# A shift that follows as a bias: the first two projection blocks from rows without the additive part of the modulation

## The chip, the cores and the metric

The kernel runs on one core of one Trainium2 chip. The metric is the device time in microseconds of one execution; lower is better. A profile of one execution is read beside it.

## The reference

A transformer block with adaptive modulation is followed by two more blocks (a short convolution mixer and a dilated attention mixer, each with its feed-forward part), on 256 tokens of width 1024 in float32. Only the start matters here:

```
mod = silu(c) @ w_ada + b_ada          # c: 1 x 1024, w_ada: 1024 x 6144
shift1, scale1, gate1, shift2, scale2, gate2 = split(mod, 6)
h    = rms_norm(x, norm1_w) * (1 + scale1) + shift1
proj = h @ w_in                        # 1024 x 2832
gq, gk, gv, gz, ga, gb, sq, sk, sv = split(proj, ...)
qkv  = silu(causal_depthwise_conv(concat([gq, gk, gv]), conv_w))   # 4 taps
```

After it come a chunked gated delta rule on q, k and v, a sliding window attention, the output projection and the feed-forward part. Scale and shift are the same for all tokens, so h @ W is (x_normed * (1 + scale1)) @ W plus the column shift1 @ W.

## The kernel before

Features lie on the partitions, tokens in the free dimension. x is eight tiles of 128 features x 256 tokens. All weights come in blocks of 1024 rows x 256 columns (1 MB), one after the other through a ring of three buffers (`raw`). For float32 accuracy each block is split: ScalarE writes a rounded high part (`hi(w)`, L650), VectorE the rest (`lo(w)`, L1017), and TensorE multiplies high by high, high by low and low by high (`three`, L1615 is the line of every product). One block of a projection is 8 row tiles x 2 column halves x 3 = 48 products.

Each engine runs its own hand-written list of instructions; semaphores join them. Around the change the order is this.

SyncE issues the two halves of x, then four transfers of modulation weights (`load_ada(0, 0..3)`), weight blocks 0 and 1, four more modulation transfers as their buffers come free (`load_ada(1, 0..3)`), and after the third of these has landed the rest of the weight blocks. A modulation transfer has half of the 1024 input rows and 512 output columns; `half` 0 are the columns for features 0 to 511, `half` 1 those for 512 to 1023, of the scale (i = 0, 1) and of the shift (i = 2, 3).

TensorE multiplies each with silu(c) (`ada`), four rows of partial results at once. ScalarE copies them to SBUF (`mod_rows_copy`, L689), and TensorE turns and sums them with products of one column (`row_sums`). VectorE makes from them the factor a1 (`first_scales`) and the shift (`first_shifts`), then for each of four row tiles `first_scaled` (times a1 plus shift), ScalarE's high part (`h_high`, L676) and the low part (`first_low`, L1069). x was multiplied by the reciprocal root mean square first (L1125).

So TensorE's order is: `ada`, sums of squares, `ada`, the root's broadcast, `ada`, `row_sums`, `ada`, `row_sums`, with ten products on zeros between (`warm`); block 0, rows 0 to 3 (`column_half`); the four products of the second half; block 1, rows 0 to 3; block 0, rows 4 to 7; the gate product `gab` and a T5 product; block 1, rows 4 to 7; then blocks 2 to 10 one by one. The first six blocks go through a causal convolution: ScalarE copies the block to `pad` (L724), VectorE does four taps on each of two tiles (L1171 the first, L1178 the others), ScalarE applies SiLU (`feature`, L712) and, for queries and keys, squares the result (L715). The second part of the modulation (gate1 and others) is not made on TensorE: VectorE accumulates eight blocks with `accumulate` (L1032, L1034), whose place in the load order stands in `MOD_AT`.

Of the kernel before, what the change touches and what calls it, by code (L numbers as in the profile page):

```python
# [43 lines left out]
MOD_AT = ((0, 8), (9, 1), (10, 1), (W_OUT, 2 + EARLY_BLOCKS), (W_OUT + 2, 2), (LOOP_W, 6 - EARLY_BLOCKS)) + tuple((FFN_BASE[0] + 3 * j + 2, 1) for j in (2, 3, 4, 5))  # L44
# [10 lines left out]
STREAM_ORDER.sort()  # L55

# [111 lines left out]
class Semaphores:  # L168


    def __init__(self, new):
# [5 lines left out]
        self.x_scaled = new("x_scaled")  # L177
# [41 lines left out]
        self.t_ready = new("t_ready")  # L219
        self.h_hi_ready = new("h_hi_ready")  # L220
# [14 lines left out]
        self.pad_ready = new("pad_ready")  # L235
        self.conv_done = new("conv_done")
# [76 lines left out]
def build(nc, stream, x_in, consts_in, vectors_in, gab_in, t5_onehot, t5_log, rel_bias, out):  # L313
    t5_scratch = nc.dram_tensor("t5_scratch", (16, 384), F32, kind="Internal")
    with ExitStack() as ctx:
# [51 lines left out]
        with ExitStack() as one:  # L367
# [14 lines left out]
            second_ident = p1("second_ident", [P, HALF])  # L382
            gab_w = p1("gab_w", [P, KD * 16])
# [149 lines left out]
        def _(sp):  # L533
# [9 lines left out]
            def load_ada(half, i):  # L543
                if half:
                    sp.wait_ge(s.ada_used, i + 1)
                k, c = 4 * (i % 2), 512 * half + (D if i < 2 else 0)
                sp.dma_start(ada_raw[i].rearrange("p (k c) -> p k c", k=4),
                             stream[k:k + 4, :, c:c + 512].rearrange("k p c -> p k c")).then_inc(ada_landed[i], 16)
# [80 lines left out]
        def _(act):  # L629
# [40 lines left out]
            def h_high(n, ks=range(KD)):  # L670
                for k in ks:
                    act.wait_ge(s.t_ready, 8 * n + k + 1)
                    if n:
                        act.activation(normed(n)[0][:, k, :], nt[:, k, :], ACT.Identity, bias=shift2[:, k:k + 1]).then_inc(s.h_hi_ready, 1)
                    else:
                        act.activation(normed(n)[0][:, k, :], nt[:, k, :], ACT.Copy).then_inc(s.h_hi_ready, 1)  # L676
# [10 lines left out]
            def mod_rows_copy(half, u):  # L687
                act.wait_ge(s.ada_used, 4 * half + 2 * u + 2)
                act.activation(mod_rows[half][u], B[u][:, :], ACT.Copy).then_inc(s.rows_copied, 1)  # L689

            mod_rows_copy(0, 0)
            r = weight_load(0)
            act.wait_ge(raw_landed[r % RING], (r // RING + 1) * 16)
            for q in range(4):
                act.activation(high_of(0)[:, 2 * q:2 * q + 2, :], raw_of(r)[:, 2 * q:2 * q + 2, :], ACT.Copy).then_inc(s.first_hi, 1)
                if q == 1:
                    mod_rows_copy(0, 1)
            hi(1)
            h_high(0, range(4))
# [3 lines left out]
            mod_rows_copy(1, 0)  # L703
            mod_rows_copy(1, 1)
            h_high(0, range(4, KD))


            dest = [kT[:, 0:2, :], kT[:, 2:4, :], qT[:, 0:2, :], qT[:, 2:4, :], vT[:, 0:2, :], vT[:, 2:4, :]]

            def feature(w):  # L710
                act.wait_ge(s.conv_done, w + 1)
                act.activation(dest[w], cacc.rearrange("p (a b) -> p a b", a=2), ACT.Silu).then_inc(s.feature_ready, 1)  # L712
                if w < 4:
                    act.wait_ge(s.feature_ready, w + 1)
                    act.activation(head_sq[w].rearrange("p (a b) -> p a b", a=2), dest[w], ACT.Square).then_inc(s.head_squared, 1)  # L715

            for w in range(6):
                hi(w + 2)
# [5 lines left out]
                act.activation(pad[:, :, 3:259], A[w % 4].rearrange("p (a b) -> p a b", a=2), ACT.Copy).then_inc(s.pad_ready, 1)  # L724
                if w:
                    feature(w - 1)
                if w == 0:
                    act.wait_ge(s.gab_product, 1)
                    act.activation(gabT, B[0][0:16, 0:T], ACT.Copy).then_inc(s.gab_copied, 1)
                if w == 2:  # L730
# [275 lines left out]
        def _(dve):  # L1006
# [56 lines left out]
            def first_scaled(k):  # L1063
                dve.wait_ge(s.x_scaled, k + 1)
                dve.tensor_scalar(nt[:, k, :], nt[:, k, :], a1[:, k:k + 1], mods[:, k:k + 1], ALU.mult, ALU.add).then_inc(s.t_ready, 1)

            def first_low(k):
                dve.wait_ge(s.h_hi_ready, k + 1)
                dve.tensor_tensor(h_lo[:, k, :], nt[:, k, :], h_hi[:, k, :], ALU.subtract).then_inc(s.h_lo_ready, 1)  # L1069

            def first_scales(half):
                c, at = slice(4 * half, 4 * half + 4), 480 + 8 * half
                dve.wait_ge(s.rows_summed, 2 * half + 1)
# [3 lines left out]
            def first_shifts(half):  # L1077
                c, at = slice(4 * half, 4 * half + 4), 484 + 8 * half
                dve.wait_ge(s.rows_summed, 2 * half + 2)
                dve.tensor_tensor(mods[:, c], STAT[:, at:at + 4], vecs("b_ada")[:, c], ALU.add).then_inc(s.mod_ready, 1)  # L1080
                dve.wait_ge(s.mod_ready, 2 * half + 2)
# [41 lines left out]
            dve.wait_ge(s.rstd_ready, 1)  # L1123
            for k in range(KD):
                dve.tensor_tensor(nt[:, k, :], x[:, k, :], B[3][:, 256:512], ALU.mult).then_inc(s.x_scaled, 1)  # L1125
# [8 lines left out]

            first_scales(0)
            first_lows((0, 1))
            first_shifts(0)
            for k in range(4):
                first_scaled(k)
                if k:  # L1140
                    first_low(k - 1)
            first_low(3)
            first_lows((2, 3))
            lo(1)
            dve.wait_ge(s.gab_hi, 1)
            dve.tensor_tensor(gab_wl[:, :], gab_w[:, :], gab_wh[:, :], ALU.subtract).then_inc(s.gab_lo, 1)
            first_scales(1)
            first_shifts(1)
            for k in range(4, KD):
                first_scaled(k)  # L1150
                if k > 4:
                    first_low(k - 1)
            first_low(KD - 1)


            for w in range(6):
# [5 lines left out]
                lo(w + 2)  # L1162
                if w < 6:
                    dve.wait_ge(s.pad_ready, w + 1)
                    if w:
                        dve.wait_ge(s.feature_ready, w)
                    tile0 = (4, 6, 0, 2, 8, 10)[w]
                    for mt in range(2):
                        o = cacc[:, 256 * mt:256 * mt + 256]
                        cw = V_AT["conv_w"][0] + 4 * (tile0 + mt)  # L1170
                        dve.tensor_scalar(o, pad[:, mt, 0:256], vec[:, cw:cw + 1], None, ALU.mult).then_inc(s.dve_step, 1)  # L1171
                        steps[0] += 1
                    for tap in range(1, 4):
                        for mt in range(2):
                            o = cacc[:, 256 * mt:256 * mt + 256]
                            cw = V_AT["conv_w"][0] + 4 * (tile0 + mt) + tap
                            dve.wait_ge(s.dve_step, steps[0] - 1)
# [8 lines left out]
                if w == 1:  # L1186
# [9 lines left out]
                if w == 2:  # L1196
# [30 lines left out]
            accumulate(at)  # L1227
            at += 1
# [8 lines left out]
            dve.tensor_scalar(v8(coefq[:, :]), hsv[:, :, 8:16], HD ** -0.5, None, ALU.mult).then_inc(s.coef_ready, 1)  # L1237

# [374 lines left out]
        def _(pe):  # L1613
# [16 lines left out]
            def column_half(w, bank, ks, after_one=None):  # L1630

                if w or ks[0]:
                    pe.wait_ge(s.lo_ready, w + 1)
                wh = high_of(w)
                wl = low_of(w)
                for k in ks:
                    if k == 1 and after_one is not None:
                        after_one()
# [4 lines left out]
                    pe.wait_ge(s.h_lo_ready, k + 1)  # L1643
# [4 lines left out]
                if ks[-1] == KD - 1:  # L1648
                    ins.then_inc(s.block_used, 1)
# [90 lines left out]
            def ada(half, i):  # L1740

                pe.wait_ge(ada_landed[i], 16 * (half + 1))
                if half and i % 2 == 0:
                    pe.wait_ge(s.rows_copied, 1 + i // 2)
# [685 lines left out]
```

## Time and profile before

| | us |
|---|---|
| median of 3 runs | 1009.4 (1009.29 to 1013.27) |
| the profiled execution | 1015.11 |
| its span, first to last instruction | 1013.3 |
| TensorE busy (matmul) | 978.1 |
| VectorE busy | 611.0 |
| ScalarE busy | 476.1 |
| mean granted clock, share of full | 0.985 |

The profiled execution is longer than the median by 5.7 us; durations below come from it. A row of a timeline gives the start, the length from the first start to the last end of a merged group, the engine, the line, what is written from what, the count, and in brackets how long the engine had been idle and what ended that. Matmul ends are modelled, so the distance between starts says more than a duration. A float32 product counts as two instructions, a product of split parts as one.

### The profile page before, as it was taken

The page shows a single profiled execution, that of the slowest core. Times are in us where ns is not written, and L with a number is a line of the kernel's source. Part 1 is how long each engine was busy: PE and PEld are TensorE (multiplying, and loading weights), DVE is VectorE, ACT ScalarE, POOL GpSimd, SP SyncE. Part 2 cuts the span into 40 slices and gives each one's busy share as a digit, 9 for nine tenths or more (in the row PEclk, how much of TensorE's full clock was granted, in tenths as well). Part 3 has the DMA queues.
Part 4 walks back from the last instruction along what each step waited for, and adds up shares of the span by engine and source line. Part 5 has one row for each costly group of instructions (what it writes and reads, how often), then busy time and mean ns, then how long its engine had stood idle before and what let it go on. Part 6 is the DMA issues. An engine that isn't in the chain of part 4 may idle for free.

```text
span 1013.3 us, 15242 instructions
## 1 busy us (share of the span) xinstructions
PE 978.1 (97%) x6518; PEld 845.1 (83%) x6518; DVE 611.0 (60%) x749; ACT 476.1 (47%) x635; POOL 35.8 (4%) x36
## 2 busy tenths in 40 slices
PE   5799999999999999999999999999999999999997
PEld 3699988988878888899878888888999878888885
DVE  2488998865656454687664536364776564545453
ACT  3376358445334344534273434345645473535342
POOL 0000542000000000000000000000000000000000
PEclk9799999989999999999999999999999999999998
DMA  9746422756675546265544555554544255454521
GB/s 344 282 154 223 167 85 90 287 209 248 233 265 216 199 142 231 84 250 183 192 164 168 185 190 187 187 190 143 208 156 142 78 188 186 163 211 170 204 83 41
DMA packets 31554, 185.66 MB, mean 183 GB/s; under 512 B 3008, under 2 KB 5504, under 8 KB 10752
## 3 DMA queue, kind: packets, MB, share of 16 engines
q1 hardware_dynamic: 29952, 180.37, 49.4%
q0 software_dynamic: 832, 3.17, 1.0%
q10 hardware_dynamic: 704, 1.17, 0.3%
q8 instruction: 51, 0.84, 0.3%
q14 instruction: 15, 0.12, 0.0%
HBM read 183.62 MB, written 1.07 MB: 182 GB/s over the span
## 4 chain that ended last, share of the span: by engine, by line
PE 78%; DVE 11%; DMA 4%; ACT 4%; issue 2%; POOL 0%; SPq 0%; ACTq 0%; DVEq 0%
PE bank L1615 42%; PE acc L1615 33%; DVE w_lo L1017 3%; ACT w_hi L650 3%; DMA raw<-stream 2%; DMA keys_queries<-stream 2%; PE bank L2197 2%; DVE XT L1178 1%; DMA AT<-stream 1%; PE bank L1979 1%; DVE h_parts L1454 0%; DVE keys_queries L1034 0%; DVE XT L1309 0%; PE acc L1715 0%; PE bank L1715 0%
## 5 line engine op out<-in xcount | busy, mean ns | idle before, releaser
L1017 DVE TENSOR_TENSOR w_lo<-raw,w_hi 128x2048 fp32r<-128x2048 f32 x145 | 329.4, 2289 | 161.3 <-ACT w_hi L650 160.8
L1615 PE MATMUL bank<-w_hi,h_parts 128*128 128x512 f32 x1056 | 334.8, 392 | 3.2 <-DVE w_lo L1017 2.4
L650 ACT ACTIVATE w_hi<-raw 128x2048 fp32r<-128x2048 f32 x145 | 272.7, 1907 | 94.0 <-PE acc L1615 62.0
L1615 PEld LDWEIGHTS bank<-w_hi,h_parts 128*128 128x128 f32 x1056 | 199.2, 189 | 46.1 <-DVE w_lo L1017 3.2
L1615 PE MATMUL bank<-w_lo,h_parts 128*128 128x512 f32 x528 | 206.2, 391 | 0.0
L1615 PE MATMUL acc<-h_parts,w_hi 128*128 128x256 f32 x928 | 174.6, 290 | 3.1 <-DVE h_parts L1069 2.1
L1615 PEld LDWEIGHTS acc<-h_parts,w_hi 128*128 128x128 f32 x928 | 147.1, 195 | 7.7 <-issue 6.1
L1615 PE MATMUL acc<-h_parts,w_lo 128*128 128x256 f32 x464 | 133.2, 287 | 0.0
L1615 PE MATMUL acc<-w_hi,o_hi 128*128 128x512 f32 x296 | 118.9, 402 | 0.0
L1615 PEld LDWEIGHTS bank<-w_lo,h_parts 128*128 128x128 f32 x528 | 99.6, 189 | 20.2
L1615 PE MATMUL acc<-w_hi,o_lo 128*128 128x512 f32 x296 | 115.6, 391 | 0.0
L1615 PE MATMUL acc<-w_lo,o_hi 128*128 128x512 f32 x296 | 115.5, 390 | 0.0
L1615 PEld LDWEIGHTS acc<-h_parts,w_lo 128*128 128x128 f32 x464 | 90.3, 195 | 0.0
L1483 DVE TENSOR_TENSOR o_lo<-bank,o_hi 128x512 fp32r<-128x512 f32 x33 | 22.8, 691 | 79.3 <-ACT o_hi L892 79.1
L887 ACT ACTIVATE silu_and_hid<-bank,rms 128x256 f32<-128x256 f32 x44 | 20.9, 475 | 104.2 <-PE bank L1615 104.2
L1615 PEld LDWEIGHTS acc<-w_hi,o_lo 128*128 128x128 f32 x296 | 55.6, 188 | 12.3
L1615 PEld LDWEIGHTS acc<-w_hi,o_hi 128*128 128x128 f32 x296 | 55.6, 188 | 10.9 <-issue 0.2
L1615 PEld LDWEIGHTS acc<-w_lo,o_hi 128*128 128x128 f32 x296 | 55.7, 188 | 10.6
L892 ACT ACTIVATE o_hi<-bank 128x512 fp32r<-128x512 f32 x33 | 19.8, 599 | 77.3 <-PE bank L2197 77.3
L1475 DVE SCALAR_TENSOR_TENSOR silu_and_hid<-bank,rms,silu_and_hid 128x256 f32<-128x256 f32 x44 | 21.2, 481 | 33.0 <-ACT silu_and_hid L887 33.0
L1615 PE MATMUL bank<-h_parts,w_hi 128*128 128x256 f32 x192 | 34.9, 286 | 0.0
L1615 PEld LDWEIGHTS bank<-h_parts,w_hi 128*128 128x128 f32 x192 | 29.7, 190 | 0.2 <-issue 0.2
(365 smaller groups left out, 973.1 us busy)
## 6 DMA issues: line engine op xcount, KB each, us to landing
raw<-stream SPq DMA_DIRECT2D x162, 1024.0 KB, 5.0
AT<-stream SPq DMA_DIRECT2D x2, 1024.0 KB, 12.0
qkT<-stream SPq DMA_DIRECT2D x2, 1024.0 KB, 11.8
X_inv<-stream SPq DMA_DIRECT2D x2, 1024.0 KB, 13.0
keys_queries<-stream SPq DMA_DIRECT2D x2, 1024.0 KB, 15.1
t_tables<-t_scratch POOLq DMA_DIRECT2D x1, 2048.0 KB, 12.1
x_res<-x_in SPq DMA_DIRECT2D x2, 512.0 KB, 5.2
t_tables<-t_scratch POOLq DMA_DIRECT2D x1, 1024.0 KB, 14.5
```

The lines of the kernel that those rows point to most:

```text
L650: act.activation(high_of(w), raw_of(r), ACT.Copy).then_inc(s.hi_ready, 1)
L887: act.activation(sg[:, T * t:T * t + T], B[t][:, 0:256], ACT.Silu, scale=rms[:, t:t + 1] if f else 1.0).then_inc(s.silu_ready, 1)
L892: act.activation(hid_parts(j)[0].rearrange("p a b -> p (a b)"), B[2][:, :], ACT.Copy).then_inc(s.hid_hi_ready, 1)
L1017: dve.tensor_tensor(low_of(w), raw_of(weight_load(w)), high_of(w), ALU.subtract).then_inc(s.lo_ready, 1)
L1178: ins = dve.scalar_tensor_tensor(out=o, in0=pad[:, mt, tap:tap + 256], scalar=vec[:, cw:cw + 1], in1=o, op0=ALU.mult, op1=ALU.add)
L1475: dve.scalar_tensor_tensor(out=o, in0=up, scalar=rms[:, t:t + 1], in1=gate, op0=ALU.mult, op1=ALU.mult).then_inc(s.hid_ready, 1)
L1483: dve.tensor_tensor(low.rearrange("p a b -> p (a b)"), B[2][:, :], high.rearrange("p a b -> p (a b)"), ALU.subtract).then_inc(s.hid_lo_rea ...
L1615: return pe.matmul(o, l, r, start=start, stop=stop, skip_group_check=True)
L1979: ins = pe.transpose(bank[hh][:, P * i:P * i + P], sc[:, hh, P * i:P * i + P], perm)
L2197: ins = pe.transpose(B[2][:, T * i + P * t:T * i + P * t + P], hid[:, T * t + P * i:T * t + P * i + P], ident)
```

## The change

It has five parts.

- The first two blocks are multiplied with "plain" rows, x times root times a1, without the shift (`first_scaled` is now one operation from x; `plain_high`, `plain_low`). TensorE also multiplies their weights with the shift (`shift_products`: two columns, the shift's high and low part, each with the high and the low part of the weights, 32 products for each block). A reduction adds these up to `first_bias`, and ScalarE adds it when it copies the two blocks to `pad`. After the last plain product (`plain_used`) ScalarE and VectorE write the rows anew with the shift in them, for all later blocks.
- The transfers come as scale, scale (features 0 to 511), block 0, scale, scale (512 to 1023), block 1, shift, shift, block 2, shift, shift. TensorE's order follows; `row_sums` works by halves of 64 columns.
- Both parts of block 2 are made before the loop over the blocks, and the gate and T5 products come after block 2.
- The first convolution tap goes from VectorE to ScalarE (`first_tap`).
- The first two loads of the second part of the modulation both stand behind block 9, and the first `accumulate` stands behind the coefficients.

```diff
-MOD_AT = ((0, 8), (9, 1), (10, 1), (W_OUT, 2 + EARLY_BLOCKS), ...
+MOD_AT = ((0, 8), (10, 2), (W_OUT, 2 + EARLY_BLOCKS), ...
@@ SyncE
-            for i in range(4):
-                load_ada(0, i)
+            load_ada(0)
+            load_ada(1)
             load(0)
+            load_ada(2)
+            load_ada(3)
             load(1)
-            for i in range(4):
-                load_ada(1, i)
-            sp.wait_ge(ada_landed[2], 32)
-            for i in range(2, len(LOADS)):
+            load_ada(4)
+            load_ada(5)
+            load(2)
+            load_ada(6)
+            load_ada(7)
+            for i in range(3, len(LOADS)):
                 load(i)
@@ ScalarE
+            def plain_high(ks):
+                for k in ks:
+                    act.wait_ge(s.t_ready, k + 1)
+                    act.activation(h_hi[:, k, :], nt[:, k, :], ACT.Copy).then_inc(s.plain_hi, 1)
...
+            plain_high(range(4))
+            mod_rows_copy(1)
             hi(1)
-            h_high(0, range(4))
+            plain_high(range(4, KD))
...
-            mod_rows_copy(1, 0)
-            mod_rows_copy(1, 1)
-            h_high(0, range(4, KD))
+            mod_rows_copy(2)
+            act.wait_ge(s.mod_ready, 3)
+            act.activation(shift_parts[:, 0:4, 0], mods[:, 0:4], ACT.Copy).then_inc(s.shift_hi, 1)
+            hi(2)
+            mod_rows_copy(3)
+            act.wait_ge(s.mod_ready, 4)
+            act.activation(shift_parts[:, 4:8, 0], mods[:, 4:8], ACT.Copy).then_inc(s.shift_hi, 1)
+            act.wait_ge(s.plain_used, 1)
+            for k in range(KD):
+                act.activation(h_hi[:, k, :], nt[:, k, :], ACT.Identity, bias=mods[:, k:k + 1]).then_inc(s.h_hi_ready, 1)
...
+            def first_tap(w):
+                act.wait_ge(s.pad_ready, w + 1)
+                for mt in range(2):
+                    cw = V_AT["conv_w"][0] + 4 * (CONV_TILES[w] + mt)
+                    ins = act.activation(cacc[:, 256 * mt:256 * mt + 256], pad[:, mt, 0:256], ACT.Copy, scale=vec[:, cw:cw + 1])
+                ins.then_inc(s.tap_ready, 1)
...
+                if w < 2:
+                    act.wait_ge(s.bias_ready, 1)
+                    for mt in range(2):
+                        ins = act.activation(pad[:, mt, 3:259], A[w][:, 256 * mt:256 * mt + 256], ACT.Identity,
+                                             bias=first_bias[:, 2 * w + mt:2 * w + mt + 1])
+                    ins.then_inc(s.pad_ready, 1)
@@ VectorE
+            first_lows((0, 1))
             first_scales(0)
-            first_lows((0, 1))
-            first_shifts(0)
+            dve.wait_ge(s.rstd_ready, 1)
             for k in range(4):
                 first_scaled(k)
...
             first_lows((2, 3))
+            first_scales(1)
+            for k in range(4, KD):
+                first_scaled(k)
+                if k > 4:
+                    plain_low(k - 1)
+            plain_low(KD - 1)
             lo(1)
...
+            first_shifts(0)
+            lo(2)
             first_shifts(1)
+            dve.wait_ge(s.plain_used, 1)
+            for k in range(KD):
+                first_low(k)
+            dve.wait_ge(s.block_used, 2)
+            dve.tensor_reduce(first_bias[:, :], A[3][:, 0:8].rearrange("p (n two) -> p n two", two=2), AX.X, ALU.add).then_inc(s.bias_ready, 1)
@@ TensorE
+            def shift_products(w, ks):
+
+                wh, wl = high_of(w), low_of(w)
+                pe.wait_ge(s.shift_lo, ks[-1] // 4 + 1)
+                for k in ks:
+                    for mt in range(2):
+                        c, o = slice(P * mt, P * mt + P), A[3][:, 4 * w + 2 * mt:4 * w + 2 * mt + 2]
+                        mm(o, wh[:, k, c], shift_parts[:, k, :], w + k + mt == 0, False)
+                        ins = mm(o, wl[:, k, c], shift_parts[:, k, :], False, k == KD - 1)
+                return ins
...
+            ada(0)
             sums(0)
+            ada(1)
             rstd(0)
+            row_sums(0)
+            ada(2)
             warm(4)
+            column_half(0, A[0], range(4))
+            ada(3)
+            warm(2)
+            row_sums(1)
             warm(6)
+            column_half(0, A[0], range(4, KD))
+            ada(4)
+            ada(5)
+            column_half(1, A[1], range(4))
+            row_sums(2)
+            ada(6)
+            ada(7)
+            column_half(1, A[1], range(4, 6))
+            shift_products(0, range(4))
+            row_sums(3)
+            column_half(1, A[1], range(6, KD)).then_inc(s.plain_used, 1)
+            shift_products(1, range(4))
+            shift_products(0, range(4, KD)).then_inc(s.block_used, 1)
+            shift_products(1, range(4, KD)).then_inc(s.block_used, 1)
```

## Rows read from the trace of the kernel before

**Rows 1.** The page: TensorE's busy time, its clock by slices, the chain's shares.
```profile
PE 978.1 (97%) x6518; PEld 845.1 (83%) x6518; DVE 611.0 (60%) x749; ACT 476.1 (47%) x635; POOL 35.8 (4%) x36
...
PEclk9799999989999999999999999999999999999998
...
PE 78%; DVE 11%; DMA 4%; ACT 4%; issue 2%; POOL 0%; SPq 0%; ACTq 0%; DVEq 0%
```

**Rows 2.** TensorE's waits, 0 to 140 us: total us, times, longest.
```profile
PE bank L1615 <- DMA AT<-stream: 10.5, 1, 10.5
PE bank L1615 <- DMA keys_queries<-stream: 2.2, 1, 2.2
PE acc L1615 <- DVE h_parts L1069: 2.1, 1, 2.1
PE bank L1615 <- DMA X_inv<-stream: 0.9, 1, 0.9
PE bank L1615 <- DVE coefq L1237: 0.7, 1, 0.7
```

**Rows 3.** Timeline of TensorE, 20 to 57 us: start, length, group, idle before.
```profile
20.33 1.05 PE L1615 MATMUL bank<-consts,inv_b 128*128 128x1 f32 x8
...
28.31 0.40 PE L1615 MATMUL acc<-h_parts,w_hi 128*128 128x256 f32 x2
...
28.67 0.40 PE L1615 MATMUL acc<-h_parts,w_hi 128*128 128x256 f32 x2
...
31.77 1.04 PE L1615 MATMUL bank<-qkT,c_columns 128*32 128x512 f32 x8
...
34.70 1.05 PE L1615 MATMUL bank<-consts,inv_b 128*128 128x1 f32 x8
37.93 1.93 PE L1615 MATMUL bank<-keys_queries,c_columns 128*32 128x512 f32 x8 [2.18 <-DMA keys_queries<-stream]
...
41.24 1.70 PE L1615 MATMUL bank<-consts,inv_b 128*128 128x1 f32 x8
42.80 0.78 PE L1615 MATMUL acc<-h_parts,w_hi 128*128 128x256 f32 x2
...
49.80 0.40 PE L1615 MATMUL bank<-h_parts,gab_wh 128*16 128x256 f32 x2
...
53.45 0.51 PE L1615 MATMUL acc<-h_parts,w_hi 128*128 128x256 f32 x2
...
56.71 0.51 PE L1615 MATMUL acc<-h_parts,w_hi 128*128 128x256 f32 x2
```

**Rows 4.** Timeline of TensorE near 198 us: one-column products.
```profile
197.79 2.03 PE L1615 MATMUL bank<-consts,keys_queries 128*64 128x1 f32 x64
```

**Rows 5.** Busy time by stretches of 2 us; PEclk, DMA share and GB/s last.
```profile
36.00:38.00 2.00, 0.07 (x4) 0.07 (x8) 0.15 (x1) 0.00 (x0) 0.00 (x0) 0.72 1.01 422
...
46.00:48.00 2.00, 2.00 (x14) 2.00 (x14) 0.62 (x2) 1.74 (x1) 0.00 (x0) 0.72 0.00 0
...
198.00:200.00 2.00, 2.00 (x66) 1.99 (x63) 1.69 (x4) 1.70 (x2) 0.00 (x0) 1.00 0.01 4
200.00:202.00 2.00, 2.00 (x14) 2.00 (x14) 1.28 (x2) 2.00 (x2) 0.00 (x0) 0.68 0.03 8
...
204.00:206.00 2.00, 2.00 (x19) 2.00 (x18) 1.26 (x1) 0.00 (x0) 0.00 (x0) 0.96 0.97 287
```

**Rows 6.** Timeline of VectorE, 42 to 97 us.
```profile
42.98 0.16 DVE L1080 TENSOR_TENSOR mods<-bank,vec 128x4 f32<-128x4 f32 x1 [6.83 <-PE bank L1615]
...
55.09 2.29 DVE L1017 TENSOR_TENSOR w_lo<-raw,w_hi 128x2048 fp32r<-128x2048 f32 x1 [1.47 <-ACT w_hi L650]
59.25 0.62 DVE L1171 TENSOR_SCALAR XT<-inv_p,vec 128x256 f32<-128x256 f32 x2 [1.87 <-ACT keys_queries L712]
59.78 2.46 DVE L1178 SCALAR_TENSOR_TENSOR XT<-inv_p,vec,XT 128x256 f32<-128x256 f32 x6
...
96.10 0.69 DVE L1241 TENSOR_TENSOR keys_queries<-keys_queries,bank 128x512 f32<-128x512 f32 x1 [1.20 <-PE bank L1615]
```

More of the change, by code:

```diff
@@ L219, in __init__ @@
         self.t_ready = new("t_ready")
+        self.plain_hi = new("plain_hi")
+        self.plain_lo = new("plain_lo")
+        self.plain_used = new("plain_used")
+        self.shift_hi = new("shift_hi")
+        self.shift_lo = new("shift_lo")
+        self.bias_ready = new("bias_ready")
         self.h_hi_ready = new("h_hi_ready")
@@ L235, in __init__ @@
         self.pad_ready = new("pad_ready")
+        self.tap_ready = new("tap_ready")
         self.conv_done = new("conv_done")
@@ L672, in h_high @@
                     act.wait_ge(s.t_ready, 8 * n + k + 1)
[L673 to L676, printed above, removed]
+                    act.activation(normed(n)[0][:, k, :], nt[:, k, :], ACT.Identity, bias=shift2[:, k:k + 1]).then_inc(s.h_hi_ready, 1)
             act.wait_ge(s.vectors_loaded, 16)
@@ L1628, in three, with column_half @@
                 return mm(o, wl, xh, False, last)
-            def column_half(w, bank, ks, after_one=None):
-                if w or ks[0]:
-                    pe.wait_ge(s.lo_ready, w + 1)
+            def column_half(w, bank, ks):
                 wh = high_of(w)
                 wl = low_of(w)
+                if w:
+                    pe.wait_ge(s.lo_ready, w + 1)
                 for k in ks:
-                    if k == 1 and after_one is not None:
-                        after_one()
                     if w == 0 and k in (0, 2, 4):
@@ L1738, in _, with ada, row_sums @@
             two = lambda b: b[:, :].rearrange("p (a b) -> p a b", a=2)
[L1740 to L1744, printed above, removed]
+            def ada(i):
+                pe.wait_ge(ada_landed[i % 4], 16 * (i // 4 + 1))
+                if i >= 4 and i % 2 == 0:
+                    pe.wait_ge(s.rows_copied, i // 2 - 1)
                 for k in range(4):
-                    ins = mm(B[i // 2][32 * k:32 * k + 32, :], c_columns[:, 4 * (i % 2) + k, :],
-                             ada_raw[i][:, 512 * k:512 * k + 512], i % 2 == 0, i % 2 == 1)
+                    ins = mm(B[i // 2 % 2][32 * k:32 * k + 32, :], c_columns[:, 4 * (i % 2) + k, :],
+                             ada_raw[i % 4][:, 512 * k:512 * k + 512], i % 2 == 0, i % 2 == 1)
                 ins.then_inc(s.ada_used, 1)
-            def row_sums(half, u):
-                pe.wait_ge(s.rows_copied, 2 * half + u + 1)
-                if half + u:
-                    pe.wait_ge(s.mod_ready, 2 * half + u)
+            def row_sums(q):
+                pe.wait_ge(s.rows_copied, q + 1)
+                if q:
+                    pe.wait_ge(s.mod_ready, q)
                 for j in range(4):
-                    at = 480 + 8 * half + 4 * u + j
-                    ins = mm(STAT[:, at:at + 1], mod_rows[half][u][:, P * j:P * j + P], ones, True, True)
+                    at = 480 + 4 * q + j
+                    ins = by_halves(STAT[:, at:at + 1], mod_rows[q // 2][q % 2][:, P * j:P * j + P], ones, True, True)
                 ins.then_inc(s.rows_summed, 1)
```

135 lines of the change are left out of this document (58 added, 77 removed).

## The prediction

> **What bounds the kernel now.** I read the page first: TensorE is busy for 97% of the span and holds 78% of the chain of waits, and the clock row has its lowest digit, 7, in the second slice, 25 to 51 us [rows 1]. So the end moves only if TensorE does less, waits less or runs less at its lower clock. Next the waits of TensorE in the first 140 us: 10.5 us before the first transfer lands, 2.1 us for the first rows of h, 0.9 and 2.2 us for later shift and scale weights, and 0.7 us before the row scales; no others of note [rows 2]. Then its timeline. It waits until 37.93 for the last of eight transfers of modulation weights. From there it is dense to 94.3, but at half clock until about 47: eight one-column products take 1.70 us at 41.24 and 1.05 us at 20.33 [rows 3]. The clock table agrees, 0.72 in 36 to 38 and again in 46 to 48 [rows 5], which puts the fall at 36.9 and the return at 47.1 (1.1 of 2 us at half). The change works on this stretch. Before, block 2 starts at 56.71, with the small gate products and the T5 product (49.80 to 53.45, 3.65 us) already done [rows 3].
>
> What follows moves with that start: each block is 48 products at 0.119 us (16 groups, 28.31 to 28.67 each), 5.7 us on TensorE [rows 3]; VectorE needs 2.3 + 0.6 + 2.5 = 5.4 us per block [rows 6]. Only DVE's coefficients make TensorE wait, 0.7 us [rows 2].
>
> **The change, part by part.**
>
> *Scales first.* Block 0's first rows now need two of the eight modulation transfers instead of four, and no shift. Behind the sums (15.9), the second transfer and the root, row_sums(0) ends near 20 and a1 near 20.8. VectorE then makes rows 0 to 3, one product and one subtraction per row, each like a tap of the same width (2.46/6 = 0.41 us [rows 6]), 0.8 us a row, from 20.8 to 24.2. TensorE's first half ends near 25, against 30.9 before. The third quarter's sums follow at 27.4, rows 4 to 7 run 28.2 to 32.0, and block 0 is done (plain) near 32.8. The 2.1 us wait and the two later DMA waits shrink. But this does not move the end by itself, because the shift weights are still needed.
>
> *The last transfer.* The queue gets the weights of block 2 ahead of the last two modulation pieces. They carry 1.05 MB, and the queue moves 422 GB/s at that time [rows 5], so the last piece lands 2.5 us later than 37.93: 40.4. (The constants' transfer moves by some 3 us on ScalarE's queue; the same bytes are ahead either way.) TensorE reaches this point near 39.4: two pieces of 1.04 us [rows 3] after 32.8, the low parts of block 1 ready at 34.3, half a block 2.9, sums 0.5, one piece 1.1. It waits 1.0 us, and ends the last piece at 41.5.
>
> *What is left then.* Half of block 1: 8 groups of 0.357, 2.9 us. row_sums(3) by halves: 0.5. And the new part: 64 products of 128x128 weights with two columns. No row shows this shape. Below, 64 half-wide one-column products take 2.03 us, 0.032 each [rows 4]: 64 cost 2.0. Above, full-wide one-column products at the low clock start every (42.80 - 41.24)/8 = 0.195 us: 12.5 us [rows 3]. The nearest row has the same weights at the high clock: 1.05/8 = 0.13, or 0.12 from start to start: 7.7 us [rows 3]. I take that. Block 2 then starts at 41.5 + 2.9 + 0.5 + 7.7 = 52.6. The 3.65 us of gate and T5 products come after it, so 56.3 stands against 56.7: **-0.4 us** at a clock that never falls.
>
> The Trainium skill's page "TensorE: Matmul & The Clock Gate" says under "LDWEIGHTS" that loading takes the number of weight columns over 1.2 GHz, 107 ns here. Its section "Back-to-back issue gap" gives a floor of 25 ns for few columns, by which 64 products would be 1.6 us (an estimate from that page). The row at 20.33 speaks for the first, since its one-column products are also four times as far apart as 25 ns.
>
> *The clock.* At 197.79 TensorE ran 64 one-column products, never idle: busy 2.00 of 2.00 us. The granted clock fell to 1.2 GHz near 200.6, 2.8 us after they began, though wide products had already resumed, and came back near 204.1 [rows 4, 5]. The changed kernel has 16 two-column products (1.9 us) and row_sums(3) together at 43.0 to 45.5, then 1.4 us of wide ones, and then 48 two-column products in a row. By that row the clock falls near 46, 2.8 us after the first of them, and I take it to stay down through the 48. The 48 then cost 48 x 0.195 = 9.4 instead of 5.8: +3.6. After them it takes as long to come back as from 200.6 to 204.1, 3.5 us of wide products at half rate: +1.75. Together **+5.3**. This replaces a loss which was inside the 56.7 of before (36.9 to 47.1).
>
> The same page's table "Why this matters for your kernels" asks only for work without idle gaps between bursts. By that rule the clock would stay up here and the sum be -0.4; the trace differs, 2.03 us of gapless narrow work preceding a fall. That is the first rival below.
>
> *The rows with the shift.* Eight ScalarE operations and eight DVE ones (8 x 0.41, about 4 us with the first latency) lie beside the 48 products (5.8 us). Block 2 takes its row tiles in turn, 0.71 us each, and waits only for the first, ready some 0.9 us after the last plain product; so even products at 0.032 each (1.5 us) would hide them. ScalarE's and DVE's new wait for the last plain group (plain_used, 46.9) has behind it these rows and then the evictions of blocks 0 and 1, which need the bias anyway. The bias reduction and two 256-wide evictions instead of one wide one add 0.3 + 0.2 us to the first convolution, which has slack of a block. Cost 0, bounds 0 and +1.
>
> *Low and high parts of block 2* (2.3 and 1.9 us) move ahead of the bias on DVE and ScalarE, beside waiting time (DVE idled 6.83 us there [rows 6]). Cost 0. ScalarE's wait for gab_product stands one block later; behind it queue the high parts of block 4, due a whole block later. Cost 0, at most +1.
>
> *The tap.* DVE loses 0.62 us a block, six times; ScalarE gains two operations, about 0.7 us. Pad, SiLU and tap now stand in a row (2.0 us) beside DVE's 2.3 us of low parts. The round falls from 5.4 to some 4.8 us, but TensorE's 5.7 stays above both: 0. Bounds: -0.7, the wait before the row scales, to +1.
>
> *The first accumulation* (1.27 us) leaves the path to the head statistics for DVE's 1.20 us gap at 96.10 [rows 6]. The loads of two blocks change places, a block ahead of use. I count -0.3 of the 0.7 us wait.
>
> **Sum.** -0.4 + 5.3 - 0.3 = +4.6 us. The profiled execution took 1015.1 us (span 1013.3), which would be 1019.7; the median of three is 1009.4, the profile lying 5.7 above it, so the forecast is **1014.0 us**. From 95 us on nothing differs, and both VectorE's and TensorE's work moves with the start.
>
> **Rivals.**
> - *The clock stays up* (20%). The row at 197.79 has half-wide weights; with full-wide ones the clock may not answer in the same way. Then -0.4 - 0.3: 1008.7. Against it: eight full-wide ones from 34.70 on, and waiting, came before the fall at 36.9. For it: those at 20.33 brought none [rows 3].
> - *Products at 0.032 us* (10%), and no fall. 2.0 in place of 7.7 us: -0.4 - 5.7 - 0.3 = -6.4, 1003.0. This is the faster side; it is faster by 5 us once a product costs less than 7.7 - 4.3 = 3.4 us by 64, 0.053. For it stands only the half-wide row; against it the full-wide row at the same clock.
> - *The clock falls in the first 16 products* (10%) and all that follows is slow: +1.4 for the half block and +1.7 more afterwards, 1017.1.
>
> The forecast keeps 60%. About 0.5%, 5 us, is what a measurement can tell from no change, and the forecast lies right at it. I put 0.26 of its 0.60 beyond it. Slower: 0.26 + 0.10 = 0.36. Faster: 0.10. Within: 0.54. Range 1004.5 to 1018: the cheap products' case and a tail above stay out.
>
> **What would show it.** In the new trace: the first block's products starting near 22 us; the last modulation transfer used near 40.4; 64 two-column products with a pitch of 0.12 or 0.195; the granted clock at 0.50 from about 46 into block 2; block 2's first product near 56 (by the sum, 52.6 + 3.6); a DVE round of 4.8 us; coefficients near 99. A pitch near 0.03, or a clock of 1.00 through 43 to 60, makes the prediction wrong.

## The result and the profile after

| | before | after |
|---|---|---|
| median, us | 1009.55 (1009.29 to 1013.27, 4 runs) | 1017.51 (1015.51 to 1019.08, 4 runs) |
| the profiled execution | 1015.11 | 1019.08 |
| its span | 1013.3 | 1017.3 |
| mean granted clock | 0.985 | 0.987 |

The ratio is 1.0072, with a 95% interval of 1.0051 to 1.0092: slower by 5.1 to 9.3 us, against a forecast of +4.6, which lies just below that interval. The two profiled executions lie only 4.0 us apart. That of before lost more behind the front part: its first SiLU of the feed-forward part starts at 230.52, in after it starts at 236.93, 6.4 us later, and what follows takes 782.8 and 780.4 us. So I compare stretches of the traces up to there, and medians for the whole.

The page of after. TensorE is busy 8.4 us longer with 98 more recorded instructions, and the digit 7 of the clock's second slice [rows 1] is gone: the lowest of the front part is now the 8 of the third slice, 50.9 to 76.3 us:

```profile
PE 986.5 (97%) x6616; PEld 851.9 (84%) x6616; DVE 609.9 (60%) x740; ACT 485.9 (48%) x659; POOL 35.7 (4%) x36
...
PEclk9989999989999999999999999999999999999999
...
PE 77%; DVE 10%; ACT 5%; DMA 4%; issue 2%; POOL 0%; SPq 0%; ACTq 0%; DVEq 0%
```

TensorE's waits, 0 to 140 us. The 2.2, 0.9 and 2.1 us of before [rows 2] are down to 0.4; a new one of 1.0 us stands behind the coefficients:

```profile
PE bank L1665 <- DMA AT<-stream: 10.7, 1, 10.7
PE bank L1934 <- DVE keys_queries L1291: 1.0, 1, 1.0
PE acc L1665 <- DVE h_parts L1113: 0.4, 1, 0.4
PE bank L1665 <- DVE coefq L1284: 0.2, 1, 0.2
```

TensorE's timeline. The last modulation piece (41.45) waits for nothing. The shift products stand 0.112 us apart at first and 0.213 us apart near 53; block 2 starts at 56.00 and block 3 at 67.20. In before, block 2 starts at 56.71 [rows 3] and block 3, sixteen groups later, at 62.51:

```profile
20.03 1.93 PE L1665 MATMUL bank<-X_inv,c_columns 128*32 128x512 f32 x8
21.90 2.08 PE L1665 MATMUL acc<-zero_r 128*128 128x512 f32 x4
23.77 0.63 PE L1665 MATMUL acc<-h_parts,w_hi 128*128 128x256 f32 x2
...
41.45 1.04 PE L1665 MATMUL bank<-keys_queries,c_columns 128*32 128x512 f32 x8
...
43.97 0.25 PE L1665 MATMUL acc<-shift_parts,w_lo 128*128 128x2 f32 x1
44.08 0.25 PE L1665 MATMUL acc<-shift_parts,w_hi 128*128 128x2 f32 x1
44.20 0.25 PE L1665 MATMUL acc<-shift_parts,w_lo 128*128 128x2 f32 x1
...
53.22 0.35 PE L1665 MATMUL acc<-shift_parts,w_lo 128*128 128x2 f32 x1
53.44 0.35 PE L1665 MATMUL acc<-shift_parts,w_hi 128*128 128x2 f32 x1
...
56.00 0.77 PE L1665 MATMUL acc<-h_parts,w_hi 128*128 128x256 f32 x2
...
63.58 0.40 PE L1665 MATMUL bank<-h_parts,gab_wh 128*16 128x256 f32 x2
...
67.20 0.51 PE L1665 MATMUL acc<-h_parts,w_hi 128*128 128x256 f32 x2
```

The stretches of 2 us, columns as in [rows 5]. TensorE is busy all the time. The clock falls within 46 to 48, is full again from 50 to 52, in the middle of the narrow products, falls once more near 53.1 and stays at half until 60:

```profile
44.00:46.00 2.00, 2.00 (x27) 1.99 (x26) 1.22 (x1) 0.00 (x0) 0.00 (x0) 1.00 0.00 0
46.00:48.00 2.00, 2.00 (x20) 1.98 (x19) 0.33 (x2) 0.21 (x1) 0.00 (x0) 0.57 0.92 246
48.00:50.00 2.00, 2.00 (x13) 2.00 (x12) 0.14 (x1) 0.76 (x2) 0.00 (x0) 0.57 0.69 287
50.00:52.00 2.00, 2.00 (x20) 2.00 (x19) 2.00 (x6) 2.00 (x6) 0.00 (x0) 1.00 0.00 0
52.00:54.00 2.00, 2.00 (x16) 2.00 (x15) 1.11 (x3) 0.56 (x2) 0.00 (x0) 0.78 0.00 0
54.00:56.00 2.00, 2.00 (x12) 2.00 (x11) 0.00 (x0) 0.00 (x0) 0.00 (x0) 0.50 0.00 0
...
58.00:60.00 2.00, 2.00 (x12) 2.00 (x11) 1.65 (x5) 2.00 (x2) 0.00 (x0) 0.51 0.00 0
60.00:62.00 2.00, 2.00 (x18) 2.00 (x18) 2.00 (x4) 1.13 (x4) 0.00 (x0) 1.00 0.01 4
```

VectorE near the coefficients. The row scales follow the accumulation without a gap; the low parts of block 10 (106.66) then come late:

```profile
97.10 2.29 DVE L1060 TENSOR_TENSOR w_lo<-raw,w_hi 128x2048 fp32r<-128x2048 f32 x1 [2.33 <-ACT w_hi L665]
...
99.39 0.17 DVE L1284 TENSOR_SCALAR coefq<-head_stat 128x16 f32<-128x16 f32 x1
99.47 1.28 DVE L1075 TENSOR_SCALAR inv_b<-raw,c_act_sb 128x2048 f32<-128x2048 f32 x1
100.76 0.69 DVE L1291 TENSOR_TENSOR keys_queries<-keys_queries,bank 128x512 f32<-128x512 f32 x1
...
106.66 2.29 DVE L1060 TENSOR_TENSOR w_lo<-raw,w_hi 128x2048 fp32r<-128x2048 f32 x1 [1.20 <-ACT w_hi L665]
```

The reason is one step further back, on ScalarE, which waits for the load of block 10 (0.30 us in the trace of before, 2.60 here; the first row is of before, the second of after):

```profile
97.21 1.92 ACT L650 ACTIVATE w_hi<-raw 128x2048 fp32r<-128x2048 f32 x1 [0.30 <-DMA raw<-stream]
104.70 1.92 ACT L665 ACTIVATE w_hi<-raw 128x2048 fp32r<-128x2048 f32 x1 [2.60 <-DMA raw<-stream]
```

### The profile page after: what moved, and what is told of

It is laid out like the page before. It is cut to its first block, busy times and chain, and to the rows that moved or that the text cites. A ratio compares the mean times of both kernels' runs of the same rounds, so it can differ in the third digit from the quotient of the medians.

```text
span 1017.3 us, 15460 instructions
## 1 busy us (share of the span) xinstructions
PE 986.5 (97%) x6616; PEld 851.9 (84%) x6616; DVE 609.9 (60%) x740; ACT 485.9 (48%) x659; POOL 35.7 (4%) x36
## 4 chain that ended last, share of the span: by engine, by line
PE 77%; DVE 10%; ACT 5%; DMA 4%; issue 2%; POOL 0%; SPq 0%; ACTq 0%; DVEq 0%
PE bank L1665 40%; PE acc L1665 33%; ACT w_hi L665 3%; DMA raw<-stream 3%; DVE w_lo L1060 3%; PE bank L2259 2%; DMA AT<-stream 1%; DVE XT L1227 1%; DVE keys_queries L1077 1%; PE bank L2041 1%; DVE h_parts L1504 0%; DVE XT L1359 0%; PE acc L1773 0%; PE bank L1773 0%; DVE soft L1379 0%
```

## The experiments

All ran in 5 rounds beside the kernel before, e3_tap_dve and e4_acc_back 6 times and the others 12 times (medians of before 1010.25 us with e1, e2, e4, e5; 1009.75 with e3, e6, e7, e8; 1010.55 with e9 to e12). A ratio compares a kernel with the runs of before in its own rounds and says more than the difference of two medians. The marks are from one profiled execution of each kernel, in us: start of block 3, end of the chain to the coefficients (start of `coefq`), VectorE's first product after the attention matrix (AT), first SiLU of the feed-forward part (FFN). The kernels e1, e2, e8 and e12 leave the shift out of the first two blocks; they are there to price its products.

| | median | ratio, 95% interval | block 3 | coefq | AT | FFN |
|---|---|---|---|---|---|---|
| before | 1009.55 | | 62.5 | 94.74 | 118.69 | 230.52 |
| after | 1017.51 | 1.0072 (1.0051 to 1.0092) | 67.20 | 99.39 | 124.60 | 236.93 |
| e1_wide | 1013.48 | 1.0027 (1.0011 to 1.0043) | 62.6 | 95.10 | 119.93 | 231.83 |
| e2_none | 1012.39 | 1.0012 (0.9995 to 1.0029) | 56.2 | 90.91 | 118.38 | 231.93 |
| e3_tap_dve | 1017.56 | 1.0073 (1.0050 to 1.0097) | 63.5 | 96.75 | 121.48 | 231.78 |
| e4_acc_back | 1017.16 | 1.0056 (1.0034 to 1.0078) | 65.0 | 98.16 | 122.12 | 235.70 |
| e5_fill_gap | 1011.28 | 0.9999 (0.9982 to 1.0015) | 61.5 | 93.76 | 117.73 | 229.19 |
| e6_row | 1014.01 | 1.0035 (1.0020 to 1.0050) | 60.4 | 94.42 | 119.15 | 229.41 |
| e7_row_acc | 1012.92 | 1.0028 (1.0014 to 1.0043) | 59.9 | 94.91 | 120.47 | 232.31 |
| e8_none_acc | 1009.94 | 0.9998 (0.9985 to 1.0011) | 57.0 | 92.72 | 118.35 | 229.52 |
| e9_before_coef | 1009.35 | 0.9984 (0.9969 to 1.0000) | 61.8 | 90.06 | 117.25 | 230.51 |
| e10_row_coef | 1009.98 | 0.9994 (0.9979 to 1.0009) | 59.6 | 90.63 | 117.03 | 228.90 |
| e11_row_coef_tap | 1010.27 | 0.9998 (0.9982 to 1.0013) | 59.6 | 90.71 | 118.04 | 228.41 |
| e12_none_coef_tap | 1008.18 | 0.9977 (0.9963 to 0.9991) | 55.9 | 88.02 | 114.69 | 228.03 |

**e1_wide: the same number of products, wide ones.**

```diff
-                        mm(o, wh[:, k, c], shift_parts[:, k, :], w + k + mt == 0, False)
-                        ins = mm(o, wl[:, k, c], shift_parts[:, k, :], False, k == KD - 1)
+                        mm(A[3][:, 0:256], wh[:, k, c], zero_r[:, 0:256], True, True)
+                        ins = mm(A[3][:, 0:256], wl[:, k, c], zero_r[:, 0:256], True, True)
```

> The changed kernel with each of the 64 two-column products replaced by one of 256 columns on the same weights with zeros as the moving side, so the bias is zero. Theory (the clock): the profile after shows the clock at half in 46.3 to 49.4 and from 53.1 to 60.0, 10 us at half. Wide products start as far apart as two-column ones (0.119 against 0.112), so their count costs the same, but the clock stays up: block 2 starts near 51.4 instead of 56.0, and the time falls by 5 us, to 1012.5. Rival (the products cost only by their number): block 2 starts at 56 or later and the time stays at 1017.5.

Two stretches of its trace and its products:

```profile
46.00:48.00 2.00, 2.00 (x20) 2.00 (x17) 0.33 (x2) 0.48 (x2) 0.00 (x0) 1.00 0.76 311
...
54.00:56.00 2.00, 2.00 (x19) 2.00 (x19) 0.40 (x2) 1.97 (x5) 0.00 (x0) 1.00 0.00 0
```

```profile
52.75 0.28 PE L1665 MATMUL acc<-zero_r,w_hi 128*128 128x256 f32 x1
52.87 0.28 PE L1665 MATMUL acc<-zero_r,w_lo 128*128 128x256 f32 x1
```

A product of 256 columns takes 0.12 us from start to start, little more than one of 2 (0.112), and the clock stays at 1.00. Block 3 starts 4.65 us earlier than in after, the median is 4.0 us lower and the ratio 0.45% (the two intervals don't touch). So the narrowness itself costs some 4 us, through the clock, and it saves nothing to speak of in return.

**e2_none: no shift products.**

```diff
-                for k in ks:
...
+                return mm(A[3][:, 0:8], wh[:, 0, 0:P], zero_r[:, 0:8], True, True)
```

> The changed kernel with the shift products left out (one tiny product on zeros in place of each group of 16, the bias is zero). Theory: 64 products of 0.112 us (7.2) and the clock's 5 us go, but the rows with the shift, hidden beside them so far, hold block 2 until 0.9 us after the last plain product: block 2 starts near 46.5 to 47 and the time falls by 9 us, to 1008.5, which is about the kernel before. Rival (the end is set by VectorE's and ScalarE's convolution rounds, not by TensorE): less than 4 us of it arrives.

Block 3 starts 6.4 us before that of e1_wide (64 products at 0.12 us would be 7.6; 1.1 us of it has turned into a wait for the first shifted row), but the coefficients only 4.2 us and AT 1.6 us earlier, and the time is 1.1 us less. Something behind block 3 swallows most of what TensorE wins. One part is this row of ScalarE, the same load as in after with a longer wait:

```profile
96.89 1.92 ACT L665 ACTIVATE w_hi<-raw 128x2048 fp32r<-128x2048 f32 x1 [4.10 <-DMA raw<-stream]
```

**e3_tap_dve: the first tap back on VectorE.**

```diff
-                if w < 5:
-                    act.wait_ge(s.feature_ready, w + 1)
-                    first_tap(w + 1)
...
+                        dve.tensor_scalar(o, pad[:, mt, 0:256], vec[:, cw:cw + 1], None, ALU.mult).then_inc(s.dve_step, 1)
```

> The changed kernel with the first convolution tap back on VectorE. Theory: TensorE sets the pace of the convolution stretch (5.7 us a block against VectorE's round of 4.8 with the tap gone and 5.4 with it), so the time stays within 1 us of 1017.5. Rival (the end of the round, head statistics and coefficients, hangs on VectorE's chain): six taps of 0.6 us come back, up to +3 us, 1020.

1017.56 against 1017.51: the tap is worth nothing that these runs can tell. (Its profiled execution was its fastest, 1013.5 with a clock of 0.95 between 30 and 64 us where after had 0.85: the fall is not equally long in every execution, and the marks of this row come from a short one.)

**e4_acc_back: load order and first accumulation as before.**

```diff
-MOD_AT = ((0, 8), (10, 2), (W_OUT, ...
+MOD_AT = ((0, 8), (9, 1), (10, 1), (W_OUT, ...
...
             lo(8)
             at = MOD_START[1]
+            accumulate(at)
+            at += 1
```

> The changed kernel with the first accumulation and the load of its block put back where they were before. Theory: in the profile after, TensorE waits 1.0 us near 111 for a VectorE product that stands behind the moved accumulation, and only 0.2 us instead of 0.7 for the coefficients; so putting it back gains 0.5 us, 1017.0. Rival (the prediction's): the move filled a gap of VectorE and putting it back costs 0.3 us.

From the coefficients to AT it takes 23.96 us, as in before (23.95); after takes 25.2. The 1.0 us wait behind the coefficients is gone, but the one for them is 1.1 us. The ratio is 0.16% lower than that of after, within both intervals.

**e5_fill_gap: the kernel before with its early fall of the clock removed.**

```diff
             ada(1, 1)
+            warm(4)
             ada(1, 2)
             row_sums(1, 0)
+            warm(9)
             ada(1, 3)
```

> The kernel before, with 4 and 9 more wide products on zeros where TensorE waits for the last two modulation transfers (0.9 and 2.2 us). Theory: the fall of the clock at 36.9 follows these waits and the narrow row sums between them; without the waits the clock stays up through 37 to 47, and the time falls by up to 5 us, to about 1005 to 1006. Rival (the narrow row sums alone bring the fall): no change, 1009.5.

The clock row of 36 to 38 and that of 46 to 48 both come to 1.00, from 0.72 [rows 5]:

```profile
36.00:38.00 2.00, 2.00 (x13) 0.71 (x13) 0.00 (x0) 0.60 (x1) 0.00 (x0) 1.00 1.01 420
46.00:48.00 2.00, 2.00 (x19) 2.00 (x19) 1.30 (x4) 1.76 (x3) 0.00 (x0) 1.00 0.04 8
```

Block 3 is 1.0 us earlier, and the ratio is 0.9999. That is not what the fall of the clock is worth. In this execution TensorE came to the last modulation piece only at 41.16, against 37.93 in before [rows 3]:

```profile
30.51 0.63 PE L1615 MATMUL acc<-h_parts,w_hi 128*128 128x256 f32 x2
...
41.16 1.06 PE L1615 MATMUL bank<-keys_queries,c_columns 128*32 128x512 f32 x8
```

Most of this delay lies ahead of the fillers: the first half block starts at 30.51 instead of 27.88. From the last piece to block 3 it takes 20.4 us instead of 24.6, so full clock gives back 4.2 us there. The ratio holds this gain, the fillers and the late start together, and the run does not settle what the kernel before would take without the fall.

**e6_row and e7_row_acc: the same shift, the operands changed over.** The two columns of the shift become the stationary side and 256 weight columns move: 32 wide products instead of 64 narrow ones. e7_row_acc has the edit of e4_acc_back as well.

```diff
-                        mm(o, wh[:, k, c], shift_parts[:, k, :], w + k + mt == 0, False)
-                        ins = mm(o, wl[:, k, c], shift_parts[:, k, :], False, k == KD - 1)
+                    mm(o, shift_parts[:, k, :], wh[:, k, :], w + k == 0, False)
+                    ins = mm(o, shift_parts[:, k, :], wl[:, k, :], False, k == KD - 1)
...
+            def bias_columns():
+                pe.wait_ge(s.shift_row, 1)
+                for j in range(4):
+                    ins = mm(STAT[:, 496 + j:497 + j], shift_row[:, P * j:P * j + P], ones[0:2, :], True, True)
```

> The changed kernel with the shift products turned round: the shift (two columns, high and low part) is the stationary side and 256 columns of weights the moving one, 32 wide products in place of 64 narrow ones; ScalarE copies the two rows of results, and four products of one column turn them into the bias, behind the first two row tiles of block 2. Theory: the clock stays up as with 64 wide products on zeros (which gave 1013.5), and 32 of them, 3.8 us, go as well: block 3 starts near 58.8, the time is 1009.5 to 1010. Rival (a stationary side of two columns counts as narrow work for the clock): the clock falls after them, half of the gain is lost, 1013 to 1014.

> The same with the first accumulation and its load put back. Theory: coefficients near 92 and no wait for the weights of block 10 (2.6 us on ScalarE in the profile after), so the first masked products of AT start near 116 against 118.7 before: 1007.5 to 1008.5, below the kernel before. Rival (the start is not what ends last, VectorE's chain is): the same time as the kernel before, 1010.

Both missed. The products are as cheap as expected (0.113 us apart, 3.6 us in all) and the clock stays at 1.00 up to 64 us, so they beat after by 3.5 and 4.6 us. But block 3 is 2.1 and 2.7 us earlier than in before and the time some 4 and 3 us longer: the earlier start isn't passed on.

**e8_none_acc: no shift products, load order as before.** Edits of e2_none and e4_acc_back.

> The changed kernel with the shift products left out and the first accumulation and its load put back. Theory: without the shift products the coefficients are ready at 91.9 and the wait for block 10's weights (4.1 us with the products left out alone) goes, so 3 to 4 us less than the 1012.4 of that kernel: 1008.5. It is the most that the early rows can give. Rival (the clock's falls later in that run cost it the time): 1012.

Block 3 starts 5.5 us before that of before, the coefficients 2.0, AT 0.3, and the ratio is 0.9998. Even at no price for the shift the change gains nothing. VectorE and ScalarE in e7_row_acc show what the coefficients wait for:

```profile
90.16 0.35 DVE L1285 RECIPROCAL head_stat<-head_stat 128x32 f32<-128x32 f32 x1
92.62 2.29 DVE L1065 TENSOR_TENSOR w_lo<-raw,w_hi 128x2048 fp32r<-128x2048 f32 x1 [2.10 <-ACT w_hi L668]
94.83 0.17 DVE L1290 TENSOR_TENSOR coefk<-beta,head_stat 128x16 f32<-128x16 f32 x1
```

```profile
90.55 0.23 ACT L800 ACTIVATE head_stat<-head_stat 128x32 f32<-128x32 f32 x1 [0.98 <-DVE head_stat L1285]
90.68 1.90 ACT L668 ACTIVATE w_hi<-raw 128x2048 fp32r<-128x2048 f32 x1
```

Their operand, the root, is there at 90.8. But in VectorE's list the low parts of block 9 stand ahead of them, and these wait for ScalarE's high parts, which follow the root. TensorE pays twice, with a wait and then with the clock, which falls behind it (0.61 in 96 to 98, 0.53 in 98 to 100). e8_none_acc has the same wait of 2.0 us and the same fall (0.50 in 94 to 96):

```profile
95.14 2.46 PE L1669 MATMUL bank<-consts,coefk 128*64 128x128 f32 x32 [1.97 <-DVE coefq L1291]
97.37 1.93 PE L1669 MATMUL bank<-consts,coefq 128*64 128x128 f32 x16
```

**e9 to e12: the coefficients ahead of the low parts of block 9.** e9_before_coef has this alone on the kernel before, e10_row_coef has it on e7_row_acc, e11_row_coef_tap also has the edit of e3_tap_dve; e12_none_coef_tap is e11 with no shift products.

```diff
-            lo(9)
             hsv = hs[:, 2, :].rearrange("p (t c) -> p t c", t=TT)
             dve.wait_ge(s.head_rms, 1)
             dve.tensor_tensor(v8(coefk[:, :]), ...
             dve.tensor_scalar(v8(coefq[:, :]), ...
+            lo(9)
```

> The kernel before, with one thing moved: VectorE makes the head coefficients (two 0.17 us operations) ahead of the low parts of block 9 instead of behind them. In the trace of before, VectorE stood idle for 2.10 us (90.35 to 92.45) waiting for ScalarE's high parts of block 9 while the root of the head sums was ready at 90.6; the coefficients came at 94.74 and TensorE waited 0.7 us for them. Theory (the order of VectorE's list, not the work, holds TensorE there): coefficients near 90.8, the wait of 0.7 us gone, 0.7 us less in all, ratio near 0.9993. Rival: the next step (VectorE's row scales behind the low parts) takes the wait over, and the time is the same to 0.2 us.

> e7_row_acc (32 wide shift products, load order and first accumulation as before) and VectorE's head coefficients ahead of the low parts of block 9. e7_row_acc kept TensorE's clock and had its block 3 start 2.5 us earlier than before, yet was no faster; TensorE waited 2.0 us for the coefficients. Theory (an earlier TensorE only meets the fixed order of VectorE and ScalarE): the wait of 2.0 us goes, the first products of the delta rule come 2 us earlier, and the time is 2 us under e7_row_acc: 1011 beside 1010 for before. Rival (something in the later part holds it): same time as e7_row_acc, 1013.

> e10_row_coef with the first convolution tap back on VectorE (two operations of 0.31 us there in place of two of 0.46 us on ScalarE, per block). Theory: with TensorE early, ScalarE's row of table loads, pad, SiLU, tap and square is gapless from 61 to 79 us and sets the convolutions; without its tap the wait for kds of 0.7 us goes, 0.5 to 1 us less than e10_row_coef. Rival (VectorE's round of 5.4 us again sets the head sums): 1 us more than e10_row_coef.

> The shift products are left out altogether (no bias from them), the load order and the first accumulation are as before, VectorE's coefficients stand ahead of the low parts of block 9 and the first tap is on VectorE again. It bounds what earlier rows can give here. Theory (only the order of the other engines kept e8_none_acc at the time of before): TensorE's wait of 2.0 us for the coefficients goes, block 2 starts 5 us earlier than before's and the time is 1007.5 to 1008, ratio near 0.998. Rival (the chain over VectorE and ScalarE has no room left): 1010 again, with another wait of TensorE in place of that for the coefficients.

In e10_row_coef the wait is gone, and the narrow stretch runs at full clock:

```profile
90.63 0.17 DVE L1290 TENSOR_SCALAR coefq<-head_stat 128x16 f32<-128x16 f32 x1
```

```profile
92.83 1.97 PE L1669 MATMUL bank<-consts,coefk 128*64 128x128 f32 x32
94.62 1.04 PE L1669 MATMUL bank<-consts,coefq 128*64 128x128 f32 x16
```

AT comes 3.4 us earlier than in e7_row_acc: 2.0 us of wait and 2.46 - 1.97 + 1.93 - 1.04 = 1.4 us of slow products (block 3 had 0.25 us of it already, and a new wait of 0.2 us behind the coefficients takes as much). The median is 2.9 us lower, 0.34% by the ratios, and the two intervals don't touch. On the kernel before the same edit brings AT 1.4 us forward, of which block 3 had 0.7 already and the wait for the coefficients was 0.7; its time is 0.16% lower with an interval that ends at 1.0000. The tap (e11) is again worth nothing that can be told: 0.3 us the other way, well inside the interval. e12 is the only one clearly below before, by 2.3 us, and it has no shift products; with them, 32 wide ones, the change comes out even.

## Why the prediction was right, and where it was not

- **The place and the mechanism held.** Forecast and measured: products 0.12 and 0.112 us apart; fall of the clock near 46 and at 46.3; block 2 near 56 and at 56.00; coefficients near 99 and at 99.39. The clock rival (1008.7) and that of cheap products (1003.0) are excluded by the 0.57 and 0.50 of the clock rows and by the pitch. The third rival's figure, 1017.1, is nearest to the 1017.5 measured, but not for its reason: it had the clock fall in the first 16 products, and the record has 1.00 through all of them (44 to 46). The 1017.5 lies 0.5 us inside the range.
- **The clock's +5.3 was right in size for this one execution, which is luck, and not in shape.** I had it down from 46 through all 48 products and 3.5 us more. It was at half from 46.3 to 49.7 and from 53.1 to 60.0: 3.4/2 + 6.9/2 = 5.2 us. The profiled executions of e4_acc_back and e3_tap_dve, with the same 64 products, have only one fall, near 52, and by their clocks between 30 and 64 us (0.90 and 0.95) lost 3.4 and 1.7 us. What the width costs is better read from e1_wide, which keeps everything else: 4.65 us in the trace and 4.0 us in the median. The Trainium skill's page "TensorE: Matmul & The Clock Gate" advises under "Why this matters for your kernels" against idle gaps between bursts; here TensorE was busy 2.00 of 2.00 us in each of these rows, so that advice would not have foreseen the fall.
- **The last transfer was no wait.** I had it land at 40.4 with TensorE waiting 1.0 us. TensorE got there itself only at 41.45. The first half block started at 23.77 and not near 22, because TensorE still ran at half pace: the modulation piece at 20.03 and the four products on zeros at 21.90 took 1.87 us each, start to start, and the first groups 0.64 us, where in before the like took 1.0, 1.0 and 0.357:

```profile
21.31 1.07 PE L1615 MATMUL bank<-keys_queries,c_columns 128*32 128x512 f32 x8
22.31 1.20 PE L1615 MATMUL acc<-zero_r 128*128 128x512 f32 x4
23.34 0.95 PE L1615 MATMUL bank<-consts,inv_b 128*128 128x1 f32 x8
```

The last piece ended 0.9 us later than forecast. That was made up by products at 0.112 us (0.5) and by 3.2 us of clock loss ahead of block 2 instead of 3.6.

- **The +5.3 "replaces a loss which was inside the 56.7 of before".** So it was: e5_fill_gap's trace prices that loss at 4.2 us (20.4 us from the last piece to block 3 instead of 24.6). The change took one loss of some 4 us away and brought another of 5. The profile of e9_before_coef has the fall of before as well (0.50 from 38 to 46); whether every execution of before has it is not known.
- **The first accumulation, -0.3, is not borne out.** "A block ahead of use" is where it failed. The ring has three buffers, and two modulation loads now stand together ahead of block 10's, whose buffer is freed by the low parts of block 9 (99.3) instead of by an accumulation (89.9). ScalarE waited 2.60 us for that load instead of 0.30. From coefficients to AT that is +1.25 us (25.2 against 23.95; 23.96 with the old order in e4_acc_back). Ahead of the coefficients the move did give something: 0.2 us of wait in after against 1.1 in e4_acc_back, 1.0 against 2.0 in e6_row and e7_row_acc. By the traces the net is +0.3, but the ratios are 0.16% and 0.07% lower with the old order, both within the intervals: the sign is not shown.
- **"From 95 us on nothing differs"** left out this 1.25, and 0.5 us more between AT and FFN: +4.65 at the coefficients had become +6.4 at FFN. That, and the profile's distance to the median, which I took as 5.7 for both while after's lies 1.6 above its own, make the 1014.0 lower than the 1017.5 measured.
- **"What follows moves with that start"** is true for a later start and false for an earlier one. By the marks at block 3 the change is -6.4 (rows early: e2_none against before) + 6.4 (64 products: e1_wide against e2_none) + 4.65 (clock: after against e1_wide) = +4.7 us. The -6.4 holds the loss of clock that before had and e2_none had not; without its 4.2 us some 2 us are left for the early rows themselves, an estimate from these two traces. And e8_none_acc shows that of 5.5 us won at block 3 only 0.3 is left at AT. One limit was VectorE's list, with a 0.17 us operation behind a 2.3 us one that it does not need: e10_row_coef took that away and got back what its place costs. It was not the only one. e12, with block 3 at 55.9, gains only 4.0 us at AT and 2.3 us in time; where the rest of its 6.6 goes is not settled (in its trace TensorE waits 1.1 us for low parts and 1.0 us behind the coefficients).
- **The whole by ratios.** Of the 0.72%, 0.45% is the width of the products (after against e1_wide), 0.15% their number (e1_wide against e2_none), 0.14% the order of the loads and the accumulation (e2_none against e8_none_acc), and nothing is left. Each interval is 0.15 to 0.2% to either side, so only the first step is clear by itself.
- **The tap at 0** was right within what e3 and e11 can tell.

## What to carry to other kernels

When a step is moved off the weights' critical transfer at the price of new products, count these at their weights' pitch (here 0.112 us for 128 weight columns with only two moving ones), and ask what they do to the clock: turn the operands around so that the wide side moves (here 32 products at full clock for 64 that halved it). Before buying an earlier start, follow the chain to the next wait of the bounding engine and see whether the other engines' lists can be early too; a small operation parked behind a big one that waits for a third engine can eat much of it, and moving it cost nothing here. Before a run is read as the price of one thing, look in its trace for what else moved: e5_fill_gap removed the fall and still started its last modulation piece 3.2 us late. In a ring of buffers a load's time is set by whoever frees the buffer it falls on, so an exchange of two loads also changes who releases the buffer.

## What was not expected of the hardware

- The granted clock came back at 49.7, where the four wide groups of 46.3 to 49.0 had just given way to two-column products, stayed at 1.00 (50 to 52) while only these were running, and fell again near 53.1 with the same products still running.
- A product with 128 weight columns and two moving columns took 0.112 us from start to start, and one with 256 moving columns 0.12 us; at half clock the first took 0.213 us. With two weight columns and 256 moving ones (e6_row) it was 0.113 us.
- After 2.0 us of waiting, 48 products of 64 weight columns ran into a fall of the clock (e7_row_acc: 0.61 in 96 to 98; e8_none_acc: 0.50 in 94 to 96) that the same 48 after a wait of 1.1 us (e4_acc_back) or none (e10_row_coef) did not show (1.00): 1.4 us beside the 2.0.
- At the start of a run the record and the pace disagree. Block 0's first groups stand 0.64 us apart from 23.77 to 25.7, as groups do at a recorded clock of 0.50, and 0.357 us apart from then on, though the record gives 1.00 for 24 to 26. The half pace lasts to about 19.6 us in before, 25.7 in after and 31.7 in e5_fill_gap. Why it ends so differently, and why the record doesn't show it, is not settled.
